# Float32 transformer layers on one core: output and input panels at each block boundary run per token half

## The reference, cut to what matters

```python
for i in range(2):                       # layers of the first network, 272 tokens
    f1 = swiglu(rmsnorm(h, g[0]), gate, up, down)      # (silu(x@gate) * (x@up)) @ down
    h = h + 0.5 * rmsnorm(f1, g[1])
    m = attention(rmsnorm(h, g[2]))      # neighbourhood attention, then differential attention
    h = h + rmsnorm(m, g[3])
    f2 = swiglu(rmsnorm(h, g[4]), gate, up, down)
    h = h + 0.5 * rmsnorm(f2, g[5])
x = h[:, 16:]                            # 256 tokens
x = x + rms_norm(mixed(rms_norm(x)) @ w_out, g_mix_post)    # MoBA attention and mLSTM
u = square(relu(rms_norm(x) @ w_up)); x = x + rms_norm(u @ w_down, g_mlp_post)
```

## Time and profile before

| | us |
|---|---|
| median of 3 runs | 1592.48 |
| lowest, highest | 1592.34, 1601.32 |
| the profiled execution | 1599.82 |
| its span | 1597.70 |

### The profile page before, as it was taken

How to read it: one execution, slowest core, us unless ns; L and a number is a source line. 1 busy time by engine, 2 the same in 40 slices (tenths; PEclk the granted TensorE clock), 3 DMA queues, 4 the chain that set the end, 5 groups by cost and what they waited for, 6 DMA issues and landing times.

```text
span 1597.7 us, 27848 instructions
## 1 busy us (share of the span) xinstructions
PE 1526.1 (96%) x11578; PEld 1445.0 (90%) x11578; DVE 935.3 (59%) x1124; ACT 666.7 (42%) x827; POOL 168.2 (11%) x183
## 2 busy tenths in 40 slices
PE   6999989999899998999989998899998999899997
PEld 5999989968899998999989967899997987899996
DVE  5665465465766546665455465666646655777544
ACT  4443444434544434443433354444434333444432
POOL 1000029010300003000021000300003010210001
PEclk9999999999999999999999998999999987999998
DMA  7557854403355664554554401355555520355550
GB/s 222 163 181 182 221 184 159 134 28 95 114 168 177 182 192 148 167 183 141 167 168 157 160 1 35 125 185 184 167 179 160 179 94 1 106 159 184 185 185 27
DMA packets 250782, 233.55 MB, mean 146 GB/s; under 512 B 29759, under 2 KB 249844, under 8 KB 250688
## 3 DMA queue, kind: packets, MB, share of 16 engines
q1 hardware_dynamic: 250224, 231.96, 46.7%
q10 hardware_dynamic: 464, 0.25, 0.1%
HBM read 230.99 MB, written 1.12 MB: 145 GB/s over the span
## 4 chain that ended last, share of the span: by engine, by line
PE 85%; DVE 8%; ACT 2%; POOL 2%; issue 1%; DMA 1%; SPq 0%; POOLq 0%; DVEq 0%; ACTq 0%
PE acc L547 24%; PE acc L548 24%; PE acc L549 24%; DVE scaled L1360 3%; DVE rstd L1335 2%; PE aux L630 1%; PE aux L739 1%; PE aux L782 1%; POOL sq_sum L1932 1%; DVE w_lo L1330 1%; ACT w_hi L1004 1%; POOL h L1939 1%; PE acc L759 1%; DVE x_lo L1341 1%; PE aux L747 1%
## 5 line engine op out<-in xcount | busy, mean ns | idle before, releaser
L547 PE MATMUL acc<-x_hi,w_hi 128*128 128x272 f32 (+1 forms) x2432 | 701.6, 288 | 30.1 <-DVE x_lo L1341 21.6
L548 PE MATMUL acc<-x_lo,w_hi 128*128 128x272 f32 (+1 forms) x2432 | 697.1, 287 | 0.0
L549 PE MATMUL acc<-x_hi,w_lo 128*128 128x272 f32 (+1 forms) x2432 | 694.6, 286 | 0.0
L1330 DVE TENSOR_TENSOR w_lo<-raw,w_hi 128x2048 fp32r<-128x2048 f32 (+1 forms) x230 | 487.5, 2120 | 332.2 <-ACT w_hi L1004 332.2
L1004 ACT ACTIVATE w_hi<-raw 128x2048 fp32r<-128x2048 f32 (+1 forms) x230 | 406.0, 1765 | 410.1 <-PE acc L549 409.7
L547 PEld LDWEIGHTS acc<-x_hi,w_hi 128*128 128x128 f32 x2432 | 461.4, 190 | 39.9 <-issue 23.3
L548 PEld LDWEIGHTS acc<-x_lo,w_hi 128*128 128x128 f32 x2432 | 460.3, 189 | 0.4
L549 PEld LDWEIGHTS acc<-x_hi,w_lo 128*128 128x128 f32 x2432 | 460.4, 189 | 0.0
L547 PE MATMUL acc<-hid_hi,w_hi 128*128 128x272 f32 (+1 forms) x704 | 203.5, 289 | 0.0
L548 PE MATMUL acc<-hid_lo,w_hi 128*128 128x272 f32 (+1 forms) x704 | 201.5, 286 | 0.0
L549 PE MATMUL acc<-hid_hi,w_lo 128*128 128x272 f32 (+1 forms) x704 | 200.9, 285 | 0.0
(11 more groups left out here) (261 smaller groups left out, 1308.9 us busy)
## 6 DMA issues: line engine op xcount, KB each, us to landing
raw<-in_ffn_w_gate SPq DMA_DIRECT2D x44, 1024.0 KB, 5.3
raw<-in_ffn_w_up SPq DMA_DIRECT2D x44, 1024.0 KB, 5.4
raw<-in_ffn_w_down SPq DMA_DIRECT2D x32, 768.0 KB, 4.4
raw<-in_ffn_w_down SPq DMA_DIRECT2D x32, 640.0 KB, 4.3
raw<-in_w_up SPq DMA_DIRECT2D x16, 1024.0 KB, 5.4
raw<-in_w_down SPq DMA_DIRECT2D x16, 1024.0 KB, 5.1
raw<-in_na_w_qkv SPq DMA_DIRECT2D x12, 1024.0 KB, 5.1
raw<-in_da_w_qkv SPq DMA_DIRECT2D x12, 1024.0 KB, 5.1
```

What stands on the lines that cost most here:

```text
L547: nc.tensor.matmul(o, wh, xh, start=first, stop=False)
L548: nc.tensor.matmul(o, wh, xl, start=False, stop=False)
L549: return nc.tensor.matmul(o, wl, xh, start=False, stop=last)
L1330: nc.vector.tensor_tensor(w_lo[:, part, 0:nk * CW], raw[:, slot, 0:nk * CW], w_hi[:, part, 0:nk * CW].bitcast(F32), ALU.subtract).then_inc ...
```

## The change

- Buffers: `w_lo` lies on the same bytes as `raw` and overwrites it; `w_hi` has 4 slots as well. SP loads panel p when panel p - 4 has been **used**. Splitting no longer waits for a panel to be used, only for the load. `scaled` is gone: VectorE applies the gain when a group leaves PSUM (`scaled_y`).
- `FFN_PARTS` is 3, 3, 8, 8.
- Last output group: in the feed-forwards and MLP the group's first three panels run per chunk on the first token half and then on the second (`half_panel`), into two pairs of banks. The last panel of every output phase runs as four quarters: token half by half of the output columns (`last_panel`). Each quarter is squared and copied alone.
- First input panels: panels 0 and 1 of phases 2, 4 to 14 run together, chunk by chunk, first for one token half, then for the other (`first_panels`).
- The chain (sum, root, reciprocal, residual, rounding) runs per token half: `sum_half(0)` stands in the third quarter of the last panel, `sum_half(1)` two chunks into the first input panels. VectorE adds to `h` itself, two chunks at a time (`add_pair`); GpSimd's `add_branch` is gone. The 18 idle matmuls are gone. The sum of the new squares moves to the third input panel.
- The splits of input panels 0 and 1 are made two output panels earlier, those of panels 2 and 3 at the end of the boundary.
- The end: output per token half instead of per 512 columns.

```diff
-FFN_PARTS = ((0, 6), (6, 5), (11, 6), (17, 5))
+FFN_PARTS = ((0, 3), (3, 3), (6, 8), (14, 8))
+        w_lo = sb("w_lo", [P, SLOTS, FULL * CW], F32R, [cursor[0]])
         raw = sb("raw", [P, SLOTS, FULL * CW])
-        w_hi = sb("w_hi", [P, 2, FULL * CW], F32R)
-        w_lo = sb("w_lo", [P, 2, FULL * CW], F32R)
+        w_hi = sb("w_hi", [P, SLOTS, FULL * CW], F32R)
...
-                wait(sp, w_lo_ready, p - 3)
+                wait(sp, panel_used, p - 3)
...
+            def last_panel(k_, free, chunks, only, rhs_hi, rhs_lo, wait_rhs):
...
+                for part, half in enumerate(halves(tokens)):
                     for m in range(2):
+                        for q, k in enumerate(chunks):
+                            if part == 1 and m == 0 and q == 4:
+                                sum_half(k_, 0, tokens)
+                            wait_rhs(k)
+                            w = slice(q * CW + m * P, q * CW + m * P + P)
+                            mm = product(half_banks(part)[:, m, half], w_hi[:, slot, w], w_lo[:, slot, w],
+                                         rhs_hi[:, k, half], rhs_lo[:, k, half], only and q == 0, q == len(chunks) - 1)
...
+            def half_panel(n, j, free, chunks, first, rhs_hi, rhs_lo):
...
+                for q, k in enumerate(chunks):
+                    for part, half in enumerate(halves(rhs_hi.shape[2])):
+                        mm = chunk(half_banks(part)[:, :, half], p % SLOTS, q, rhs_hi[:, :, half], rhs_lo[:, :, half], k,
+                                   first and q == 0, False)
...
+            def first_panels(k_, tokens):
...
+                for part, half in enumerate(halves(tokens)):
+                    for k in range(DC):
+                        if part == 0 and k == 2:
+                            sum_half(k_ - 1, 1, tokens)
+                        pe.wait_ge(x_ready, SPLIT_IN[k_] + 8 * part + k + 1)
+                        for j in range(2):
...
+                            mm = chunk(banks(n, 0, j)[:, :, half], (ph.p0 + j) % SLOTS, k, x_hi[:, :, half], x_lo[:, :, half],
+                                       k, k == 0, k == DC - 1)
...
+            def sum_half(k_, part, tokens):
...
+                nc.tensor.matmul(ps_half[:, half], ones[:, :], sq_sum[:, 0, half], start=True, stop=False)
+                nc.tensor.matmul(ps_half[:, half], ones[:, :], sq[:, 1, 0, half], start=False, stop=False)
+                nc.tensor.matmul(ps_half[:, half], ones[:, :], sq[:, 1, 1, half], start=False, stop=True)\
+                    .then_inc(sum_ready, 1)
...
-                sum_rest(2 * k + 1, tokens_out)
-                if k < 7:
-                    keep_warm(aux[:, 0, :], 18)
...
@@ ScalarE and VectorE, output_steps: step(i, j) @@
-                    if (local + 1) % groups_of == 0:
+                    if (local + 1) % groups_of == 0 and local < last:
                         g = local // groups_of
                         act.wait_ge(panel_used, PHASES[n].p0 + local + 1)
...
+                    if local <= last - 2:
+                        high(n, i, j + 2)
+                    if local == last - 2 and k < MLP:
+                        high(n, i, j + 3)
+                        high(n, i, j + 4)
+                    if local == last:
+                        boundary(k)
...
+            def add_pair(k, part, q):
...
+                nc.vector.tensor_tensor(y[:, c, half], y[:, c, half], r, ALU.mult).then_inc(scaled_ready, 1)
+                dve.wait_ge(scaled_ready, done + 1)
+                nc.vector.tensor_tensor(h[:, c, half], h[:, c, half], y[:, c, half], ALU.add).then_inc(h_ready, 1)
...
+                quarter_y(k, 0, 0)
+                quarter_y(k, 0, 1)
+                dve.wait_ge(quarter_out, 3 * k + 2)
+                reciprocal(3 * k + 1, first)
+                quarter_y(k, 1, 0)
+                for q in range(4):
+                    add_pair(k, 0, q)
+                    if q == 2:
+                        quarter_y(k, 1, 1)
+                    if q >= 1 and k < MLP:
+                        low_part(k + 1, 2 * q - 2, 0)
+                        low_part(k + 1, 2 * q - 1, 0)
```

More of the change, by code:

```diff
@@ L273, in program @@
         ps_sum = aux[:, 3, :]
+        ps_half = aux[:, 2, :]
         reach = 2 * NT - 1 - NM
@@ L549, in product, with chunk, panel @@
                 return nc.tensor.matmul(o, wl, xh, start=False, stop=last)
-            def panel(n, i, j, a, pair, chunks, first, last, rhs_hi, rhs_lo, wait_rhs, halfway=None):
+            def chunk(o, slot, q, xh, xl, k, first, last):
+                for m in range(2):
+                    w = slice(q * CW + m * P, q * CW + m * P + P)
+                    mm = product(o[:, m, :], w_hi[:, slot, w], w_lo[:, slot, w], xh[:, k, :], xl[:, k, :], first, last)
+                return mm
+            def panel(n, i, j, free, o, chunks, first, last, rhs_hi, rhs_lo, wait_rhs, halfway=None, at=4):
@@ L553, in panel @@
                 p = i * 4 + (PHASES[n].p0 + j)
-                slot = (PHASES[n].p0 + j) % 2
                 pe.wait_ge(w_lo_ready, p + 1)
-                if first:
-                    wait(pe, acc_free, a - 1)
+                if free is not None:
+                    wait(pe, acc_free, free)
                 for q, k in enumerate(chunks):
-                    if q == 4 and halfway is not None:
+                    if q == at and halfway is not None:
                         halfway()
                     wait_rhs(k)
-                    for m in range(2):
[L563 to L566, removed]
+                    mm = chunk(o[:, :, 0:rhs_hi.shape[2]], (PHASES[n].p0 + j) % SLOTS, q, rhs_hi, rhs_lo, k,
+                               first and q == 0, last and q == len(chunks) - 1)
@@ L593, in from_x, with from_heads @@
                         for j in range(4):
-                            one(i, j)
+                            one(i, j, free(i, j))
                 for j in range(ph.panels % 4):
-                    one(bodies, j)
-            def down(n, units_before, rhs_hi, rhs_lo, parts, chunks_per_unit, tokens):
+                    one(bodies, j, free(bodies, j))
+            def from_heads(k_, tokens):
+                n = 2 * k_ + 1
                 ph = PHASES[n]
[L602 to L613, removed]
@@ new lines, in boundary @@
+            def boundary(k):
+                tokens = SUBS[k][4]
+                first, second = halves(tokens)
+                square_quarter(k, 0, 0)
+                square_quarter(k, 0, 1)
+                deviation(3 * k + 1, first)
+                square_quarter(k, 1, 0)
+                if k == MLP:
+                    square_quarter(k, 1, 1)
+                    deviation(3 * k + 2, second)
+                    return
+                for c in range(DC):
+                    high_part(k + 1, 0, c)
+                    if c == 1:
+                        square_quarter(k, 1, 1)
+                deviation(3 * k + 2, second)
+                n = 2 * k + 2
+                for c in range(DC):
+                    high_part(k + 1, 1, c)
+                    if c % 2:
+                        high(n, 0, 2, c // 2, 4)
+                for pair in range(4):
+                    square(n, pair, h[:, 2 * pair:2 * pair + 2, 0:tokens], tokens)
+                high(n, 0, 3)
+                deviation(3 * k + 3, slice(0, tokens))
+                if k + 1 not in (NA, DA, MIX, MLP):
+                    load_table(ACT.Silu)
```

452 lines of the change are left out of this document (276 added, 176 removed).

## The result

The changed kernel takes 1699.65 us (median of 4 runs, 1692.03 to 1704.07) against 1592.41 us before (median of 4, 1591.36 to 1601.32): a ratio of 1.066, 95% interval 1.060 to 1.071, so 6.6% slower. The forecast was slower, 1683 us, with 1650 to 1730 as its range. The profiled execution took 1692.03 us, 92.2 us more than the profiled one before.

A forecast was written before the change was run, and what follows sets the result against it. TensorE was taken as the bound, by matmul pace and boundary idle time. Half matmuls +157.7, boundaries -86.2, end -5.5 and new panel cut +24 gave +90 us: 1683 us against 1592.5, range 1650 to 1730.

The forecast's parts named there:

- What bounds the kernel: Whole kernel: TensorE, busy 96% of the span; its matmul pace and the boundaries' 101.4 us without a useful matmul count.
- A, the half's price: Last output groups and first input panels: each half matmul costs its weight load's 0.112 us, +157.7 us in all.
- Rival 1: Half matmuls stream at their own pace, 0.068/0.064 us each, giving 1570 us; chance 0.04.
- rival 2: Half matmuls' weight load is partly hidden, 0.090 us each, giving 1615 us; chance 0.05.
- B, the boundaries: Seven boundaries between output and input panels: 3.1 us a boundary remains, 21.5 in place of 107.7, so -86.2 us.
- C, the end: After the last matmul: 10.6 us remain in place of 15.7; with the sum leaving the last panel, -5.5 us.
- D, the new cut: Feed-forward output groups: third panel's split late by 3.1 us at entry and 1.5 twice between groups, +24 us.
- The sum: Whole kernel: 157.7 - 86.2 - 5.5 + 24 = +90 us, forecasting 1683 us against 1592.5.
- rival 4, the clock: Granted clock falls to 1.2 GHz for all half matmuls, +344 us more, giving 2027 us; chance 0.04.

## Why the prediction was right, point by point

- **What bounds the kernel, and A, the half's price.** Right: 0.112 us at both widths, 3072 x 0.112 - 186.3 = +157.8 us, and by itself, on 864 pairs, +88.8 for 88.9. The decision to take the pace of the weight load of L759, four loads, and not the streaming, carried the forecast. Rival 1 would need 0.068, rival 2 0.090. The 81 ns of the Trainium skill ("TensorE: Matmul & The Clock Gate", section Back-to-back issue gap) are not reached by these 4-byte operands: measured 112.
- **B, the boundaries.** Right in kind, a little too high. Predicted 3.1 us left each; measured 1.3 to 1.6 in the windows above, and 0.7 for the sum in the third panel with 0.4 for a bank still being emptied, some 2.5: -90 instead of -86.
- **C, the end.** Predicted 10.6 us behind the last matmul; it starts at 1679.93, which leaves 10.3 of the 1690.2.
- **D, the new cut.** Predicted 3.1 us at entry and 1.5 between groups. Measured in the phases concerned, 4.2 to 4.9 us of waits each in 4 or 5 places, the longest 2.6 to 2.8; from start to start, with what the records' overlap hides, 5 us for 6.1: about +20 for +24. What the term left out is the clock: behind two of the four entry waits it stood at 0.66 and 0.72 over 5 us (first and fourth row). The second and third row stand behind the starved split, the last behind a wait of 2.38 us for `z` in MLP's input phase.

```profile
165.00:170.00 5.00, 5.00 (x30) 0.66 0.75 167
285.00:290.00 5.00, 1.47 (x6) 0.50 0.01 3
290.00:295.00 5.00, 5.00 (x34) 0.78 0.00 0
1215.00:1220.00 5.00, 3.65 (x20) 0.72 0.25 78
1495.00:1500.00 5.00, 5.00 (x36) 0.79 0.04 13
```

- **The sum.** 157.8 - 90 - 5.5 + 20 = +82. The starved split adds 8.6, which the forecast did not have. The mixer's attention ran about 9 us faster in this profiled execution than in the one before, for its granted clock:

```profile
1297.70:1361.50 63.80, 60.06 (x260) 0.71 0.05 17
1378.20:1433.10 54.90, 50.99 (x261) 0.84 0.06 20
```

The dips of the five rows above add some 7. That makes 89 of the 92.2 measured; 3 are not accounted for. That +90 stood so close to +92.2 is in part luck: the starved split, the dips and the attention's clock were all missing from the sum and nearly cancel. From median to median it was +107. The median is 17 us above the forecast: its four executions lie 12 us apart, and the lowest is 100.7 above the lowest before.
- **The step that was weakest: rival 4, the clock.** It got 4 in 100, for all halves at once or none. It did not come in the changed kernel, so the forecast stood; but the runs show it was closer than that. A gap of 2 us at four places brings it for the halves behind them (+83 us), in one place it came behind a wait of 0.7 us, and narrower matmuls bring it with no gap. "Halves leave no stops" was the reason it stayed away, and it was true by some tenths of a microsecond. The count of matmuls in an attention said nothing on this.

## What to carry to other kernels

Cutting the moving side in two to hide a chain costs one weight load per added matmul: count them, and compare with the idle time that the chain leaves, before anything else. Here 1536 added loads cost 158 us to hide 90, while a better order at full width (two consumers side by side behind the boundary, the last panel's output columns one after the other, splits made ahead) took 54 of those 101 us without one. And where TensorE runs narrow matmuls, look at the granted clock behind each short wait: a 2 us gap, which wide matmuls recover from within 5 us, can cost ten times its length.

## What was not expected of the hardware

- **Narrow matmuls keep a fallen clock down.** Halves of 128 and 136 columns held 1.00 for 28 us and more when nothing interrupted them, and held 0.50 for about 40 us behind a gap of 1.93 us; quarters of 68 columns fell to 0.50 while busy. Full ones came back to 1.00 within about 5 us.
- **A floor independent of the moving columns, with 128 weight columns:** 0.112 us between starts for 136, 128 and 68 moving columns at full clock, 0.213 at half clock.
- **A row of GpSimd instructions can shut VectorE out to its end:** 11.87 us for a subtraction of 2.29, beside 0.7 us additions; for 2 of the 27 splits that began inside the unbroken row.
- **Left open:** why the mixer's attention runs at another clock from one execution to the next (about 9 us between the two profiled ones), whether the fall behind the 0.68 us wait comes in every execution, and what decides whether VectorE or GpSimd loses.
